# Head of a layer in one stage: latent attention's products and the scan's preparation between the input product's blocks, norms taken per token

## The reference, cut to what matters

```python
proj = h @ w_in[li]                                # (1040, 1024) @ (1024, 2368)
c_q, c_kv, k_pe, rw = _split(proj, [256, 128, 64, 1920])
# latent attention, head part
q  = (_rms_norm(c_q, q_norm) @ w_uq).reshape(B, L, 4, 128 + 64)    # q_nope, q_pe
q_pe = _rope(q[..., 128:], cos, sin)
kv = (_rms_norm(c_kv, kv_norm) @ w_ukv).reshape(B, L, 4, 128 + 128) # k_nope, v
k_pe = _rope(k_pe, cos, sin)
# scan, head part
u = rw + mu_prev * (prev - rw) + mu_next * (next - rw)    # neighbours along the tokens
r, k, v, wd_f, wd_b, ad_f, ad_b, gd = _split(u, [512, 512, 512, 64, 64, 64, 64, 128])
if li: v = v + (v_first - v) * sigmoid(v0 + (v @ v1) @ v2)
kk = heads(k * k_k); kk = kk * rsqrt(sum(kk * kk, -1) + 1e-12)      # 8 heads of 64
```

## Time and profile before

| | us |
|---|---|
| median of 3 runs | 6430.27 |
| lowest and highest run | 6429.37, 6437.29 |
| profiled execution, its own time | 6433.07 |
| span of the profiled execution | 6431.3 |

### The profile page before, as it was taken

How to read it: one execution, slowest core, us unless ns; L and a number is a source line. 1 busy time by engine, 2 the same in 40 slices (tenths; PEclk the granted TensorE clock), 3 DMA queues, 4 the chain that set the end, 5 groups by cost and what they waited for, 6 DMA issues and landing times. The chain is left out here.

```text
span 6431.3 us, 126676 instructions
## 1 busy us (share of the span) xinstructions
PE 5202.9 (81%) x55720; PEld 4263.4 (66%) x55720; DVE 3374.5 (52%) x4974; ACT 2117.7 (33%) x3870; POOL 1707.1 (27%) x1068
## 2 busy tenths in 40 slices
PE   5948988898759994966889898677994698899998
PEld 5926777777547773934677677556773576677786
DVE  4344444444758885335444444576887336554462
ACT  2322222222227772222222222216773214232231
POOL 0002222222237770101221222216872110022121
PEclk9978989898879996977999998788997799999999
DMA  3121000000326654121000000224665110233332
GB/s 98 41 72 25 19 12 18 10 12 9 112 93 229 231 200 135 43 75 23 16 14 19 10 12 9 79 98 178 228 232 167 47 33 2 82 96 112 98 92 98
DMA packets 342954, 510.72 MB, mean 79 GB/s; under 512 B 110008, under 2 KB 266040, under 8 KB 315160
## 3 DMA queue, kind: packets, MB, share of 16 engines
q1 hardware_dynamic: 298312, 463.14, 22.6%
q0 software_dynamic: 42752, 34.23, 1.8%
q10 hardware_dynamic: 1344, 5.24, 0.2%
HBM read 558.69 MB, written 110.97 MB: 104 GB/s over the span
## 5 line engine op out<-in xcount | busy, mean ns | idle before, releaser
L261 PE MATMUL ps<-w,xbT 128*128 128x512 f32 x2304 | 574.0, 406 | 87.1 <-DVE w L2160 87.1
L2160 DVE TENSOR_TENSOR w<-w,w 128x2048 fp32r<-128x2048 f32 x192 | 546.0, 2871 | 72.9 <-ACT w L2117 72.2
L261 PEld LDWEIGHTS ps<-w,xbT 128*128 128x128 f32 x2304 | 441.6, 195 | 191.7 <-DVE w L2160 99.0
L261 PE MATMUL ps<-hT,w_in 128*128 128x416 f32 (+1 forms) x2736 | 450.1, 327 | 8.9 <-DVE w_in L546 8.9
L261 PEld LDWEIGHTS ps<-hT,w_in 128*128 128x128 f32 x2736 | 447.3, 191 | 12.0 <-issue 9.5
L1293 POOL TENSOR_TENSOR lm<-Ab,consts 116x416 f32<-116x416 f32 x240 | 264.7, 1110 | 570.1 <-DVE T L1230 318.6
L2117 ACT ACTIVATE w<-w 128x2048 fp32r<-128x2048 f32 x192 | 362.5, 1937 | 95.7 <-DMA w<-in_moe_w_dram,widx 95.7
L1267 POOL TENSOR_SCALAR aa<-aa 128x416 f32<-128x416 f32 x40 | 30.4, 761 | 1311.8 <-ACT aa L1136 1311.8
L261 PE MATMUL ps<-T,lm 52*52 52x52 f32 x6400 | 220.8, 226 | 164.9 <-issue 64.4
L261 PEld LDWEIGHTS ps<-T,lm 52*52 52x52 f32 x6400 | 199.8, 140 | 186.1 <-issue 125.4
L1238 DVE TENSOR_TENSOR T<-T,ps 116x416 f32<-116x416 f32 x160 | 93.9, 587 | 413.0 <-PE ps L261 412.5
(11 more groups left out here) (430 smaller groups left out, 11616.4 us busy)
## 6 DMA issues: line engine op xcount, KB each, us to landing
w<-in_moe_w_dram SPq DMA_DIRECT2D x192, 1024.0 KB, 7.0
w_gate<-in_w_gate_dram SPq DMA_DIRECT2D x44, 512.0 KB, 3.9
w_up<-in_w_up_dram SPq DMA_DIRECT2D x44, 512.0 KB, 3.9
w_down<-in_w_down_dram SPq DMA_DIRECT2D x44, 512.0 KB, 3.6
w_in<-in_w_in_dram SPq DMA_DIRECT2D x38, 512.0 KB, 4.0
ys<-t_ys SPq DMA_DIRECT2D x20, 832.0 KB
t_h<-x SPq DMA_DIRECT2D x30, 416.0 KB
w_out<-in_w_out_dram SPq DMA_DIRECT2D x24, 512.0 KB, 11.6
```

Source lines behind the costliest of these rows:

```text
L261: made = e.matmul(out, a, b, start=start, stop=stop)
L2160: e.tensor_tensor(w.lo, w.x, w.hf, ALU.subtract).then_inc(*P.c("moe_dve").tick(li, "w13", b, k))
```

## The change

The three stages become one, `front_*`. The blocks of `u` are taken in another order (v, then the low-rank ones, then k, then r). What the second and third stage computed is cut in small numbered products, 73 in the first layer and 88 in the second; `front_order` puts up to two of them behind each group of the input product, of 57 groups, as soon as their inputs can be there, those of k first. They alternate between the PSUM banks 6 and 7, so number x waits until x-2 has been taken out. Results are put into three buffers `staged` in turn and stored from there; v is stored in five DMAs.

The norms are taken per token: instead of a sum on all partitions, `per_token` uses the squares as the stationary operand and a column of ones as the moving one (for each chunk of 104 tokens a product with one column, or two for the two heads of a k block). Root and reciprocal then work on 104 x 10 or 104 x 20 elements; `spread` brings the factors back to all partitions, with the factors, repeated 128 or 64 times, as the stationary operand and the identity as the moving one, and DVE multiplies straight from PSUM. The position part of q is computed for two heads at once (128 rows), for which the columns of `w_uq` are laid out anew ahead of the launch. `hT` and the buffers of the head move in SBUF. Nothing behind the head is changed in the code.

```diff
     out["b_spatial_2_c"] = np.ascontiguousarray(np.swapaxes(out["b_spatial_2"], -1, -2))
+    wq = out["mla_w_uq"].reshape(DEPTH, 256, 4, 192)
+    out["mla_w_uq_c"] = np.ascontiguousarray(np.concatenate(
+        [wq[..., :128].reshape(DEPTH, 256, 512), wq[..., 128:].reshape(DEPTH, 256, 256)], -1))
...
+COLS += [("u", j, 448 + 128 * j, 128) for j in (8, 9, 10, 11, 12, 13, 14, 4, 5, 6, 7, 0, 1, 2, 3)]
+BLOCK = {(kind, j): n for n, (kind, j, _, _) in enumerate(COLS)}
+LERP = ("rwkv_k_k", "rwkv_k_a", "rwkv_w0", "rwkv_w0", "rwkv_a0", "rwkv_a0")
+TO_DVE = ("scale q", "scale kv", "turn pe", "turn q", "scale k")
+def small_products(li):
+    thirds = range(3)
+    main = [(("sum q",), 7)] + [(("scale q", g), 9) for g in thirds]
+    main += [(("sum kv",), 10)] + [(("scale kv", g), 12) for g in thirds] + [(("turn pe", g), 12) for g in thirds]
+    for name in (("kn", 0), ("kn", 1), ("kn", 2), ("kn", 3), ("qp", 0), ("qn", 0), ("turn q", 0), ("qp", 1), ("qn", 1),
+                 ("turn q", 1), ("qn", 2), ("qn", 3)):
+        main += [(name + (g,), 15) for g in thirds]
+    main += [(("v", i), 15) for i in range(NT)]
+    if li:
+        for g in thirds:
+            main += [(("low", g), 27)] + [(("gate", g, j), 27) for j in range(4)]
+    keys = []
+    for j in range(4):
+        n = BLOCK["u", 4 + j]
+        keys += [(("sum k", j), 3 * n + 6)] + [(("scale k", j, g), 3 * n + 7) for g in thirds]
+    return main, keys
+def front_order(li):
+    main, keys = small_products(li)
+    count = 0
+    for at in range(3 * len(COLS)):
+        here = []
+        while len(here) < 2 or at == 3 * len(COLS) - 1:
+            if keys and keys[0][1] <= at:
+                queue = keys
+            elif main and main[0][1] <= at:
+                queue = main
             else:
+                break
+            here.append((count, queue.pop(0)[0]))
+            count += 1
+        yield divmod(at, 3) + (here,)
+def small_numbers(li):
+    return {name: x for _, _, here in front_order(li) for x, name in here}
+STAGED = [("kn", 0), ("kn", 1), ("kn", 2), ("kn", 3), ("qp", 0), ("qn", 0), ("qp", 1), ("qn", 1), ("qn", 2), ("qn", 3)]
+STAGED += [("v", i) for i in range(0, NT, 2)]
...
+            if li and name == ("v", NT - 1):
+                e.wait_ge(*P.c("frt_pe").at(li, "small", number))
+                e.wait_ge(*P.c("frt_dve").at(li, "turned", x["turn q", 1, 2]))
+                e.dma_start(m.v1, T["rwkv_v1"][li - 1].rearrange("(t p) n -> p t n", p=128)).then_inc(
+                    *P.d("frt_v_in").tick(li, "v1"))
+                e.dma_start(m.v2[0:32, :], T["rwkv_v2"][li - 1]).then_inc(*P.d("frt_v_in").tick(li, "v2"))
+                e.dma_start(m.v0, T["rwkv_v0_c"][li - 1]).then_inc(*P.d("frt_v_in").tick(li, "v0"))
+                old_values(0)
+            if name == ("gate", 0, 3):
+                old_values(1)
+            if name == ("gate", 1, 3):
+                old_values(2)
...
+def small_bank(number):
+    return 6 + number % 2
+def small_taker(P, name):
+    return P.c("frt_dve" if name[0] in TO_DVE else "frt_act")
+def front_pe(e, P, li):
+    m, rw, pe, dv, ac, prj = P.frt, P.rw, P.c("frt_pe"), P.c("frt_dve"), P.c("frt_act"), P.c("prj_pe")
+    x = small_numbers(li)
+    names = {number: name for name, number in x.items()}
+    ident = P.K["ident"][0:C, 0:C]
+    wv = m.wkv.rearrange("p (h e) -> p h e", h=4)[:, :, 128:256]
+    def per_token(ps, parts, w, what):
+        return [(ps[0:C, w * i:w * i + w], part[:, C * i:C * i + C], what, k == 0, k == len(parts) - 1)
+                for i in range(NT) for k, part in enumerate(parts)]
+    def spread(ps, parts, g):
+        t0, tn = GROUPS[g]
+        return [(ps[to, C * k:C * k + C], bc(x[0:C, t0 // C + k:t0 // C + k + 1], [C, to.stop - to.start]), ident, True,
+                 True) for k in range(tn // C) for to, x in parts]
+    for n, g, here in front_order(li):
+        w, (t0, tn) = m.w[n % 3], GROUPS[g]
+        if g == 0:
+            e.wait_ge(*P.c("prj_pool" if n % 2 else "prj_dve").at(li, "lo", n))
+        if n >= 2:
+            e.wait_ge(*P.c("prj_act").at(li, "out", n - 2, g))
+        out = P.ps[(3 * n + g) % 6][:, 0:tn]
+        mms(e, [y for k in range(8) for y in three(out, w.at(k), P.hT.at(k, slice(t0, t0 + tn)), k == 0, k == 7)]
+            ).then_inc(*prj.tick(li, n, g))
+        for number, name in here:
+            kind, ps = name[0], P.ps[small_bank(number)]
+            if number >= 2:
+                e.wait_ge(*small_taker(P, names[number - 2]).at(li, "small", number - 2))
+            if len(name) > 1:
+                t0, tn = GROUPS[name[-1]] if kind not in ("v", "gate", "sum k") else GROUPS[0]
+                cs = slice(t0, t0 + tn)
+            if kind == "sum q":
+                e.wait_ge(*ac.at(li, "square", 1))
+                mats = per_token(ps, [m.sums[0], m.sums[1]], 1, P.K["ones"][:, 0:1])
+            elif kind == "sum kv":
+                e.wait_ge(*ac.at(li, "square", 2))
+                mats = per_token(ps, [m.sums[2]], 1, P.K["ones"][:, 0:1])
+            elif kind in ("scale q", "scale kv"):
+                which = kind == "scale kv"
+                e.wait_ge(*dv.at(li, "rms", which))
+                mats = spread(ps, [(slice(0, 128), m.rt[which])], name[1])
...
+            elif kind == "sum k":
+                e.wait_ge(*ac.at(li, "square k", name[1]))
+                mats = per_token(ps, [m.sq], 2, P.K["blk"][:, 0:128:64])
+            else:
+                j = name[1]
+                e.wait_ge(*dv.at(li, "rnorm", j))
+                mats = spread(ps, [(slice(64 * o, 64 * o + 64), m.rn[j % 2][:, :, o]) for o in range(2)], name[2])
+            mms(e, mats).then_inc(*pe.tick(li, "small", number))
...
+        if (n, g) == (1, 0):
+            square(0, P.cq[:, 0, :], prj.at(li, "out", 0, 2))
+        if (n, g) == (2, 0):
+            square(1, P.cq[:, 1, :], prj.at(li, "out", 1, 2))
+        if (n, g) == (3, 0):
+            square(2, P.ckv, prj.at(li, "out", 2, 2))
+        if g == 2 and ("u", 3 + j) in BLOCK and kind == "u" and 5 <= j <= 7 or (n, g) == (BLOCK["u", 0], 2):
+            k = j - 5 if j else 3
+            if k:
+                e.wait_ge(*pe.at(li, "small", x["sum k", k - 1]))
+            else:
+                e.wait_ge(*pe.at(li, "small", x["qn", 3, 2]))
+                e.wait_ge(*P.d("pre_in").end(li))
+            e.wait_ge(*dv.at(li, "next", BLOCK["u", 4 + k]))
+            e.activation(m.sq, rw.k[:, k, :], ACT.Square, scale=rw.par[:, 0, k:k + 1]).then_inc(
+                *ac.tick(li, "square k", k))
+        if (n, g) == (BLOCK["u", 4], 1):
+            e.wait_ge(*dv.at(li, "next", BLOCK["u", 14]))
+            e.activation(P.u[:, 12, :], P.u[:, 12, :], ACT.Tanh).then_inc(*ac.tick(li, "tanh"))
+            e.activation(P.u[:, 14, :], P.u[:, 14, :], ACT.Sigmoid).then_inc(*ac.tick(li, "sigmoid"))
...
+            elif kind in ("sum q", "sum kv"):
+                which = kind == "sum kv"
+                e.activation(m.rt[which][0:C, :], ps[0:C, 0:NT], ACT.Sqrt, bias=P.K["eps"][0:C, 0:1],
+                             scale=1.0 / (128 * (2 - which))).then_inc(*ac.tick(li, "small", number))
+            elif kind == "sum k":
+                j = name[1]
+                if j >= 2:
+                    e.wait_ge(*pe.at(li, "small", x["scale k", j - 2, 2]))
+                elif li == 0:
+                    e.wait_ge(*dv.at(li, "turned", x["turn q", 1, 2]))
+                e.activation(m.rn[j % 2][0:C], ps[0:C, 0:2 * NT].rearrange("p (i a) -> p i a", a=2), ACT.Sqrt,
+                             bias=P.K["eps"][0:C, 3:4]).then_inc(*ac.tick(li, "small", number))
...
+    for n, g, here in front_order(li):
+        if g == 0 and n + 1 < len(COLS) and (n + 1) % 2 == 0:
+            half_lo(e, P, li, n + 1, prj)
+        if n and g < 2:
+            shifted(n - 1, g)
...
+            if kind in ("sum q", "sum kv"):
+                which = kind == "sum kv"
+                e.wait_ge(*ac.at(li, "small", number))
+                e.reciprocal(m.rt[which][0:C, :], m.rt[which][0:C, :]).then_inc(*dv.tick(li, "rms", which))
+            elif kind == "sum k":
+                r = m.rn[name[1] % 2][0:C]
+                e.wait_ge(*ac.at(li, "small", number))
+                e.reciprocal(r, r).then_inc(*dv.tick(li, "rnorm", name[1]))
...
+                e.scalar_tensor_tensor(rw.kk[:, j, cs], rw.k[:, j, cs], rw.par[:, 0, j:j + 1], ps[:, 0:tn], ALU.mult,
+                                       ALU.mult).then_inc(*dv.tick(li, "small", number))
...
     embed_pe(e, P)
     for li in range(DEPTH):
         over(e, P, 0, *(COMBINE if li else EMBED))
-        project_pe(e, P, li)
-        over(e, P, li, *PROJECT)
-        mla_pe(e, P, li)
-        over(e, P, li, *MLA)
-        prep_pe(e, P, li)
-        over(e, P, li, *PREP)
+        front_pe(e, P, li)
+        over(e, P, li, *FRONTS[li])
         recur_pe(e, P, li)
         over(e, P, li, *SCAN, *ATT)
         close_pe(e, P, li)

```

(15 more changed lines are left out.)

612 lines of the change are left out of this document (264 added, 348 removed).

## The result

| | before | after |
|---|---|---|
| median (lowest to highest), us | 6432.19 (6429.37 to 6437.29), 4 runs | 6247.65 (6242.86 to 6251.26), 4 runs |
| profiled execution, own time / span | 6433.07 / 6431.3 | 6250.61 / 6248.5 |

The ratio is 0.9712, 95% interval 0.9695 to 0.9729: 184.5 us less. The forecast was 6240, 7.7 us too low and within the range.

The account below looks back on a forecast made before the run. PE was taken to bound the input product and attention products, dependency chains the rest. Layer savings of 88.5 and 102.7 us, less 1 for SP, gave -190.2: 6242.9 profiled, 6240 us forecast, range 6205 to 6290.

Parts of the forecast that it names:

- What is removed, and that PE bounds the new stage: Head: all behind the input product goes, 166.4 and 200.1 us; PE then busy in 301 of 307 us.
- First layer, 307.0: First layer's head in us: 224.6 input product, 76.4 small products, 1.5 waits, 4.5 end; against 395.5 before.
- 15.8 us for the spreads of k: PE time per layer for 80 products, 160 passes, with 64 stationary and 104 moving columns, at 0.099 us each.
- side by side: Spreads of k: two heads share the array, 160 passes at half price, 7.9 us less per layer; 6224 us, chance 0.11.
- Second layer, 327.5: Second layer's head in us: 225.5 input product, 90.9 small products, 6.5 waits, 4.6 end; against 430.2 before.
- The clock as a rival: New stage: narrow products drop PE to 1.2 GHz throughout, doubling 301 and 316 us; 6857 us, chance 0.02.
- clock in the stretch is under 0.9: Sign, in the head's stretch, that the forecast is wrong; the forecast expected 1.00 there.
- Waits: PE waits added among the small products: 1.5 us in the first layer, 6.5 in the second.
- Tail: End of the head stage: last block's move, scaling and two additions stay, with PE not busy, 4.5 and 4.6 us.
- SP: Two more small loads on the SP queue ahead of the embedding's stores: 1 us in sum, between 0 and 4.
- Warm clock, 0: Scan's start: a warm PE could give back some 4 us per layer; taken as 0, with -8 as the end.
- Handshakes: Small products: two banks not free in time, each of 161 exposing 0.6 us, 97 us; 6337 us, chance 0.11.

Follow-up runs that it names:

- e1: Changed kernel with the spreads of k no longer alternating between upper and lower 64 partitions, one half running first, then the other; 6246.5 us, ratio 0.9717.
- e11: e7 with no per-token sum sharing its slot with another small product, and the sum of c_q cut into two halves; 6242.4 us, ratio 0.9704.
- e7: Changed kernel with second-layer gate products never in the slot of a per-token sum of k, but in the next free slot; 6237.2 us, ratio 0.9696.
- e3: Changed kernel with the earlier wide norms (sums on all 128 partitions, reciprocals over a group's width) put between its groups; 6200.9 us, ratio 0.9653.
- e6: e3 with small waits taken out: Tanh and Sigmoid moved, three loads and the norms' gains issued at other places, gates kept off their rank-32 product's slot; 6190.5 us.
- e5: e3 with 36 extra unread one-pass products behind the last input-product group in either layer, to keep PE warm for the scan; 6203.2 us, ratio 0.9644.
- e8: Changed kernel with all small products in bank 6, each waiting for the taker of the one before it; 6341.0 us, one run.
- e4: Changed kernel, second layer only: gate put ahead of the second per-token sum of k, and moved to a later slot for the third; 6239.5 us, one run.
- e2: Kernel before, its three stages kept, with only the norms taken per token and no interleaving; 6378.1 us, ratio 0.9934.

## Why the prediction was right

The forecast was 7.7 us low, of a gain of 184.5, and its mechanism was right. That it came so near is in part luck, as several terms were off and cancel. By its own steps:

- **What is removed, and that PE bounds the new stage**: held. PE is busy 299.35 of 305.75 and 322.74 of 332.95 us.
- **First layer, 307.0**: measured 305.75, by two errors that cancel. The 15.8 us for the spreads of k were too much: 0.099 per pass was scaled from a row with 128 moving columns and, unlike here, more stationary ones. Measured are 0.049 to 0.056, 8 to 9 us in all. That is the price of the rival "side by side", which had the price and not the reason (e1: only a quarter is the pairing). Against it stands the clock, taken as 1.00: its falls lost 5.1 us, and e11, whose first layer has none, is 3.6 shorter than e7.
- **Second layer, 327.5**: measured 332.95. The same 7 us too much for the spreads stand against 10.3 for the clock, 6.8 of it behind the sums of k. This term was missing, and it made the sum too low; 3 us of the difference stay without a place.
- **The clock as a rival**: it was priced for a whole stage, with a sign of its own ("clock in the stretch is under 0.9"), and that was too coarse: the clock fell for 3 to 7 us at a time, and the stages' means were 0.98 and 0.96. For the whole stage it was wrong; as a cost of single places it was some 15 us beside a gain of 185. That narrow products are in it is shown by e3. Why one place falls and another doesn't is not.
- **Waits**: forecast were 1.5 and 6.5 us. The parts named for the second layer are 1.5, 2.5 and two of 0.7, which add up to 5.4, and the 2.5 is 2.0 by its own terms (0.9 + 1.5 + 2.3 - 2.7). Measured were 1.5 and 2.5 + 1.5 + 1.2 = 5.2. Taking them out gave 9.3 us (e6).
- **Tail**: 4.9 and 5.1 against 4.5 and 4.6. **SP**: 1.5 us in the first layer against 1, where e3 had 0.6.
- **Warm clock, 0**: right, for a reason that the prediction didn't have: PE then waits for the load of qp (e5).
- **Handshakes**: hidden, as argued; with one bank they cost 80 us in sum (e8).
- **The Trainium skill's rule** ("TensorE: Matmul & The Clock Gate", "The mechanism") that a weight load overlaps a matmul only with other row groups, which would have added 14 us per layer: the trace disagrees, as the row had it that the prediction went by. The spreads use the same rows throughout and ran at 0.125 and 0.056 us per pass, and in the first layer's stage the loads were busy 276.83 us beside 299.35 of matmuls, in 305.75. The same section also lets a load run ahead when it goes to a background weight buffer; whether that is what happens here no row can tell.

What the prediction didn't ask is whether both halves of the change help. It had the numbers: DVE was at 62 + 35 of 307 us, so 40 us of reciprocals had room, and the norms per token were priced at 33.0 us of PE where 7 wide products cost 12.7. That the difference of 20.3 is close to e3's 19.3 and 22.9 is luck, since 7 us of it are the spreads' wrong price. The stages divide it in another way. In the first layer e11 and e3 both ran without a fall, and e11 - e3 is 301.90 - 286.42 = 15.5 us for the products; the other 3.9 are the clock. In the second layer the falls are 10.3 us against 1.7 in e3, which leaves 14.3 for the products. The expectation of e3 had 13.6 for them, from starts in the timeline.

## What to carry to other kernels

When work moves under an engine that is the bound, price all of it on that engine anew: a form that is faster in a chain (narrow products for a short reciprocal) can be the slower one there, since the engine that it relieves is free. Read the granted clock in short stretches around narrow products and behind waits; a mean of 0.96 over a stage hid some 10 us. Look at more than one execution before a fall of the clock is put down to the instruction ahead of it. When a wait at the end of a stage is filled, look at what the next stage starts with: here it was a load that could be issued a block earlier.

## What the runs showed of the hardware

- TensorE's granted clock fell to 1.2 GHz while the engine was busy without a gap: behind 3.85 us of passes with one moving column (5.23 us for a group that takes 2.99), and behind 1.84 us of two-column passes with a 32-row product behind them (6.28 us in place of 4.7). Beside lone runs of 1.8 us it didn't fall in the first layer of e11, and fell in the second. With wide products in their place it fell beside none (e3).
- Behind the same wait of 2.4 to 2.5 us for three loads the clock fell in the changed kernel, e3 (0.76) and e11, and stayed at 1.00 in e1, e4 and e7. Without the wait it stayed up as well (e6).
- In a cold stage a per-token pass takes 0.18 us (e2), at full clock 0.09 (changed kernel).
- From start to start, a pass with 64 stationary and 104 moving columns takes 0.065 us, and 0.049 when the two halves of the partitions alternate (e1); with 128 stationary columns it takes 0.107.
